# A feed-forward whose quarter products move behind six plain chunks and grow from three pairs to five

## The reference, cut to what matters

```python
def conv_gated_ffn(x, w_up, w_gate, conv_w, conv_b, w_down):
    u = x @ w_up
    g = causal_dwconv(x @ w_gate, conv_w, conv_b)
    return (jax.nn.silu(g) * u) @ w_down
...
ffn = conv_gated_ffn(x, ffn_w_up[i], ffn_w_gate[i], ffn_conv_w[i], ffn_conv_b[i], ffn_w_down[i])
ple = jax.nn.sigmoid(x @ ple_w_gate[i]) * (p[i] @ ple_w_proj[i])
x = layer_norm(DN_ALPHA * x + ffn + ple, ln_ffn_g[i], ln_ffn_b[i])
```

## Time and profile before

| what | value |
|---|---|
| median of 3 runs | 1742.17 us (1739.85 to 1743.65) |
| the profiled execution | 1736.82 us |
| its span | 1735.0 us |
| TensorE busy | 1722.2 us |
| VectorE busy | 1149.9 us |
| ScalarE busy | 898.0 us |
| DMA moved | 214.27 MB, mean 123 GB/s |

### The profile page before, as it was taken

How to read it: one execution, slowest core, us unless ns; L and a number is a source line. 1 busy time by engine, 2 the same in 40 slices (tenths; PEclk the granted TensorE clock), 3 DMA queues, 4 the chain that set the end, 5 groups by cost and what they waited for, 6 DMA issues and landing times.

```text
span 1735.0 us, 24407 instructions
## 1 busy us (share of the span) xinstructions
PE 1722.2 (99%) x9933; PEld 1430.8 (82%) x9933; DVE 1149.9 (66%) x1814; ACT 898.0 (52%) x1410; POOL 42.7 (2%) x53
## 2 busy tenths in 40 slices
PE   9999999999999999999999999999999999999999
PEld 7887999888888897777779999888898866778766
DVE  6778897644443464877697888543378866656664
ACT  7789666433332254666574665332265354534542
POOL 0000200000000000000100000000000000000000
PEclk9999999999999999999999999999999999999999
DMA  5483456755446554411124565332323221223111
GB/s 217 137 228 97 122 150 219 236 170 169 132 151 193 139 167 133 110 49 62 61 97 146 184 182 163 104 98 98 97 63 116 87 79 54 70 89 98 61 61 49
DMA packets 67247, 214.27 MB, mean 123 GB/s; under 512 B 7104, under 2 KB 7360, under 8 KB 67136
## 3 DMA queue, kind: packets, MB, share of 16 engines
q1 hardware_dynamic: 56384, 170.77, 30.2%
q0 software_dynamic: 10752, 41.95, 9.6%
HBM read 208.50 MB, written 44.04 MB: 146 GB/s over the span
## 4 chain that ended last, share of the span: by engine, by line
PE 89%; DVE 5%; ACT 4%; DMA 1%; issue 1%; SPq 0%; DVEq 0%; ACTq 0%
PE bank L620 88%; ACT tmp L1439 1%; DMA wraw<-in_wstream 1%; DVE wl L2194 1%; DVE tmp L2185 1%; ACT wh L1439 1%; ACT taps L1439 1%; PE bank L1384 0%; DVE XL L2194 0%; DVE sbl L2194 0%; DVE HL L2194 0%; ACT Y L1439 0%; ACT XH L1439 0%; DVE X L2182 0%; DVE sqr L2185 0%
## 5 line engine op out<-in xcount | busy, mean ns | idle before, releaser
L620 PE MATMUL bank<-XH,wh 128*128 128x512 f32 (+1 forms) x1424 | 526.8, 370 | 3.1 <-DVE wl L2194 1.1
L620 PE MATMUL bank<-XH,wl 128*128 128x512 f32 (+1 forms) x1424 | 517.0, 363 | 0.0
L620 PE MATMUL bank<-XL,wh 128*128 128x512 f32 (+1 forms) x1424 | 516.9, 363 | 0.0
L2194 DVE TENSOR_TENSOR wl<-wraw,wh 128x1024 fp32r<-128x1024 f32 (+1 forms) x296 | 358.1, 1219 | 232.7 <-ACT wh L1439 231.4
L1439 ACT ACTIVATE wh<-wraw 128x1024 fp32r<-128x1024 f32 (+1 forms) x296 | 309.6, 1052 | 286.6 <-PE bank L620 244.4
L620 PEld LDWEIGHTS bank<-XH,wh 128*128 128x128 f32 x1424 | 268.7, 189 | 56.1 <-issue 9.5
L620 PEld LDWEIGHTS bank<-XH,wl 128*128 128x128 f32 x1424 | 268.7, 189 | 43.0
L620 PEld LDWEIGHTS bank<-XL,wh 128*128 128x128 f32 x1424 | 269.0, 189 | 39.8 <-issue 0.7
L620 PE MATMUL bank<-HH,wh 128*128 128x256 f32 (+1 forms) x740 | 215.1, 333 | 0.0
L620 PE MATMUL bank<-HL,wh 128*128 128x256 f32 (+1 forms) x740 | 213.5, 331 | 1.4 <-DVE sqr L2185 1.4
L620 PE MATMUL bank<-HH,wl 128*128 128x512 f32 (+1 forms) x580 | 199.3, 344 | 0.0
(11 more groups left out here) (383 smaller groups left out, 2413.2 us busy)
## 6 DMA issues: line engine op xcount, KB each, us to landing
wraw<-in_wstream SPq DMA_DIRECT2D x258, 512.0 KB, 3.6
wraw<-tw SPq DMA_DIRECT2D x80, 256.0 KB, 3.1
tw<-in_w POOLq DMA_DIRECT2D x6, 2048.0 KB, 17.6
tw<-in_w POOLq DMA_DIRECT2D x6, 1536.0 KB, 11.9
tw<-in_w POOLq DMA_DIRECT2D x6, 1024.0 KB, 7.6
wraw<-in_wstream SPq DMA_DIRECT2D x22, 256.0 KB, 3.7
tw<-tw POOLq DMA_DIRECT2D x2, 2048.0 KB, 10.5
tw<-in_w POOLq DMA_DIRECT2D x6, 512.0 KB, 5.8
```

Of the source, the lines that this page charges most:

```text
L620: return pe.e.matmul(o, l, r, start=start, stop=stop, skip_group_check=True)
L2194: return dve.e.tensor_tensor(o, x, h.bitcast(F32), ALU.subtract)
```

## The change

In the first layer six plain chunks (0 to 5) come first, then five pairs (chunks 6 to 15), then six plain chunks (16 to 21). The second layer keeps seven pairs from the start. Two pairs more are done in quarter products; the stream grows from 309 units to 315, and the first layer's up and gate hold units 42 to 101, with the pairs in 54 to 88. In the first layer the two sets of three banks are exchanged: up uses 3 to 5, gate 0 to 2. The rows of `tw` are counted through both layers: 10 for the first and 14 for the second. The first layer's are summed in three parts (4, 3 and 3 rows, from `w_lo` 15, 36 and 44, step 1) in place of two (4 and 2), the second's as before in 6 and 8 rows, from `w_lo` 64 step 4 and 104 step 5 (before 60 and 100). The first pair's products wait for the products of chunks 4 and 5 in place of the sigmoids of the side gate. The places of the summed inputs stay the same.

```diff
-PAIRS = (3, 7)
-
-SUMMED = [(0, 0, 4, 15, 1), (0, 4, 6, 36, 1), (1, 0, 6, 60, 4), (1, 6, 14, 100, 5)]
-XS0 = 14
+BEFORE, PAIRS = (6, 0), (5, 7)
+UP_BANK = (3, 0)
+
+SUMMED = [(0, 4, 15, 1), (4, 7, 36, 1), (7, 10, 44, 1), (10, 16, 64, 4), (16, 24, 104, 5)]
...
+def chunk(layer, p):
+
+    return BEFORE[layer] + 2 * p
+
+
 def ffn_order(layer):
     out = []
+    for f in range(BEFORE[layer]):
+        out += [(f"up{layer}", k, f) for k in range(KD)] + [(f"gate{layer}", k, f) for k in range(KD)]
     for p in range(PAIRS[layer]):
-        f, (up, gate), (tu, tg) = 2 * p, (f"up{layer}", f"gate{layer}"), (f"tu{layer}", f"tg{layer}")
+        f, (up, gate), (tu, tg) = chunk(layer, p), (f"up{layer}", f"gate{layer}"), (f"tu{layer}", f"tg{layer}")
...
+def row(layer, p, g):
+
+    return 2 * (pairs_before(layer) + p) + g
+
+
+def summed_in(n):
+
+    return [q for q, (n0, n1, *_) in enumerate(SUMMED) if n0 <= n < n1][0]
...
-                sp.wait_ge(s.tw, 128 * (summed_in(layer, 2 * p + (mat[1] == "g")) + 1))
-                src = a["tw"][k // 4, layer, 2 * p + (mat[1] == "g")]
+                n = row(layer, p, mat[1] == "g")
+                sp.wait_ge(s.tw, 128 * (summed_in(n) + 1))
+                src = a["tw"][k // 4, n]
...
+        sets = [bank[b:b + 3] for b in (UP_BANK[layer], 3 - UP_BANK[layer])]
+        for f in range(f0):
+            bu, bg = bank[(2 + 2 * f) % 6], bank[gate_bank(f)]
+            if f < 3:
+                pe.wait_ge(s.pg_u, 8 * layer + 4 + 2 * f)
+            else:
+                pe.wait_ge(s.f_h, FT * layer + f - 2)
+            for k in range(KD):
+                block(f"up{layer}", k, f, bu[:, :], XH[:, k, :], XL[:, k, :], k == 0, k == KD - 1)
+            if f >= 3:
+                pe.wait_ge(s.f_conv, FT * layer + f - 2)
+            for k in range(KD):
+                block(f"gate{layer}", k, f, bg[:, :], XH[:, k, :], XL[:, k, :], k == 0, k == KD - 1)
...
-            b = bank[3 * g:3 * g + 3]
+            b = sets[g]
             if p:
                 pe.wait_ge(s.u_e, 4 * (pairs_before(layer) + p - 1) + 2 * g + 2)
+            elif f0:
+                pe.wait_ge(s.f_h, FT * layer + f0 - 1 + g)
             else:
                 pe.wait_ge(s.pg_u, 8 * layer + 4 + 2 * g)
...
+        for f in range(BEFORE[layer]):
+            feed_group(up, range(KD), [f])
+            feed_group(gate, range(KD), [f])
+            act.wait_ge(s.stream, w.done(gate, KD - 1, f))
+            bias(f, bank[gate_bank(f)])
+            silu(f)
+            high(f)
...
+        for f in range(BEFORE[layer]):
+            feed_group(up, range(KD), [f])
+            feed_group(gate, range(KD), [f])
+            taps(f, bank[gate_bank(f)])
+            product(f, bank[(2 + 2 * f) % 6])
+            low(f)
```

More of the change, by code:

```diff
@@ L799, in first_products @@
             mat = ("up", "gate")[g] + str(layer)
-            product(mat, 2 * p, 0, b[0][:, lo], plain(0, lo), True, False)
-            product(mat, 2 * p, 4, b[0][:, hi], plain(4, lo), False, True)
+            product(mat, chunk(layer, p), 0, b[0][:, lo], plain(0, lo), True, False)
+            product(mat, chunk(layer, p), 4, b[0][:, hi], plain(4, lo), False, True)
         def summed_products(g, p):
-            b = bank[3 * g:3 * g + 3]
+            b = sets[g]
             mat = ("tu", "tg")[g] + str(layer)
@@ L818, in last_product @@
             pe.wait_ge(s.xs_l, 4 * layer + 4)
-            product(("up", "gate")[g] + str(layer), 2 * p + 1, 4, bank[3 * g + 1][:, lo], sums_of(3), False, True)
+            product(("up", "gate")[g] + str(layer), chunk(layer, p) + 1, 4, sets[g][1][:, lo], sums_of(3), False, True)
         for p in range(PAIRS[layer]):
@@ L1534, in ffn, with sum_high @@
         HH = m.HH[layer]
+        sets = [bank[b:b + 3] for b in (UP_BANK[layer], 3 - UP_BANK[layer])]
+        def sum_high(j):
+            act.wait_ge(s.xs_f, 4 * layer + j + 1)
+            for k0, x in m.XSG[layer][j]:
+                ins = fn(x[:, :, 0:256], m.SF[layer][j][:, k0:k0 + x.shape[1], :], ACT.Copy)
+            ins.then_inc(s.xs_h, 1)
         for f0 in (0, 4):
@@ L1614, in ffn @@
         second_out(1, tg, last)
-        for f in range(2 * PAIRS[layer], FT):
+        for f in range(chunk(layer, PAIRS[layer]), FT):
             feed_group(up, range(KD), [f])
-            if f == 2 * PAIRS[layer]:
+            if f == chunk(layer, PAIRS[layer]):
                 pair_bias(last, 0)
@@ L2349, in ffn, with sum_low @@
         lo, hi, xs = slice(0, 256), slice(256, 512), m.SF[layer]
+        sets = [bank[b:b + 3] for b in (UP_BANK[layer], 3 - UP_BANK[layer])]
+        def sum_low(j):
+            dve.wait_ge(s.xs_h, 4 * layer + j + 1)
+            for k0, x in m.XSG[layer][j]:
+                ins = less(x[:, :, hi], xs[j][:, k0:k0 + x.shape[1], :], x[:, :, lo])
+            ins.then_inc(s.xs_l, 1)
         a11, a21, a12, a22 = (X[:, k0:k0 + 4, ts] for k0 in (0, 4) for ts in (lo, hi))
@@ L2391, in first_combined @@
         def first_combined(g, p):
-            b, (o, _) = bank[3 * g:3 * g + 3], (m.ub[layer][p], m.gb)[g]
+            b, (o, _) = sets[g], (m.ub[layer][p], m.gb)[g]
             dve.wait_ge(s.u_e, 4 * (pairs_before(layer) + p) + 2 * g + 1)
@@ L2397, in three_combined @@
         def three_combined(g, p):
-            b, (o, q) = bank[3 * g:3 * g + 3], (m.ub[layer][p], m.gb)[g]
+            b, (o, q) = sets[g], (m.ub[layer][p], m.gb)[g]
             dve.wait_ge(s.u_e, 4 * (pairs_before(layer) + p) + 2 * g + 2)
@@ L2406, in last_combined @@
             q = (m.ub[layer][p], m.gb)[g][1]
-            dve.wait_ge(s.stream, w.done(("up", "gate")[g] + str(layer), KD - 1, 2 * p + 1))
-            tt(q[:, lo], bank[3 * g + 1][:, lo], q[:, lo], ALU.subtract).then_inc(s.u_c, 1)
+            dve.wait_ge(s.stream, w.done(("up", "gate")[g] + str(layer), KD - 1, chunk(layer, p) + 1))
+            tt(q[:, lo], sets[g][1][:, lo], q[:, lo], ALU.subtract).then_inc(s.u_c, 1)
+        for f in range(BEFORE[layer]):
[4 more added lines that the diff above has]
+            low(f)
         for p in range(PAIRS[layer]):
-            f = 2 * p
+            f = chunk(layer, p)
             if p:
@@ L3225, in weight_sums @@
     def weight_sums(part):
-        layer, n0, n1, at, step = SUMMED[part]
-        t1, t3, t4, t2 = (a["tw"][t, layer, n0:n1].rearrange("n p c -> (n p) c") for t in range(4))
-        w11, w12, w21, w22 = (a[n][layer, n0:n1].rearrange("n p c -> (n p) c") for n in ("w11", "w12", "w21", "w22"))
+        n0, n1, at, step = SUMMED[part]
+        t1, t3, t4, t2 = (a["tw"][t, n0:n1].rearrange("n p c -> (n p) c") for t in range(4))
+        w11, w12, w21, w22 = (a[n][n0:n1].rearrange("n p c -> (n p) c") for n in ("w11", "w12", "w21", "w22"))
         done = 8 * part
@@ L3236, in gpsimd_program @@
     for i in (1, 3):
-        for part in ((0,), (1, 2, 3))[i // 2]:
+        for part in ((0,), range(1, len(SUMMED)))[i // 2]:
             weight_sums(part)
```

61 lines of the change are left out of this document (33 added, 28 removed).

## The result

The changed kernel takes 1754.46 us (median of 5 runs, 1748.82 to 1756.43), the kernel before beside it 1740.73 us; the ratio is 1.0083 (95% interval 1.0066 to 1.0100). Five further runs of the same kernel, beside more runs of the kernel before, gave 1.0102 (1.0085 to 1.0119). It is slower by 14 us, and by 20 us in those further runs, where the forecast was +3.1 us with a range that ended at 1751. The profiled execution took 1756.43 us, its span is 1754.6 us against 1735.0. The spans differ by 19.6 us and so by more than the first medians do, since the profiled execution of before (1736.82 us) was faster than all five of its runs, and this one was the slowest of its five.

The account below looks back on a forecast made before the run. TensorE was taken to bound the kernel. Saved columns -3.2, old entry gap -1.4, new entry +1.1 and additions +6.6 gave +3.1 us: 1745.3 us from a median of 1742.17, range 1738 to 1751.

Parts of the forecast that it names:

- What bounds the kernel: Whole run: TensorE, busy 1722.2 of 1735.0 us; other engines' work costs time only where TensorE starts to wait for it.
- saved columns: First layer's pairs: each saves 1.60 us against two plain chunks; five in place of three save 3.20 us.
- what the pairs add: More splits, combinations and tails on ScalarE and VectorE beside TensorE; they fit in spare time, costed at nothing.
- the banks: Exchanged banks in the first layer: products waited for are over before the pair's products start; cost nothing.
- the exit: From pair 4 to a plain chunk: the same waits as the old exit, which cost nothing.
- The entry: Start of pairs: old gap of 1.4 us goes; new one behind chunk 5 costs 1.1 us (0 to 3).
- The weight sums beside the pairs: Layer 1's sums in pairs 1 to 4: three additions at 2.2 us each, 6.6 us (4.2 to 9); copies 0.
- (c): Rival: DMA bounds pairs 1 to 4, 0.37 us a unit; +6.5 us, 1748.7 us, up to 1751; chance 0.20.
- (a): Rival: buffers cover late landings in the pairs and the new entry is free; -4.6 us, 1737.6 us; chance 0.17.
- (b): Rival: additions fall mostly on parts of a pair without a tight drain, 1 us each; 1741.7 us; chance 0.28.
- (d): Rival: the entry behind chunk 5 costs 4 us or more on top, some 1748 us; chance 0.05.
- The signs: Expected in the trace: 1 us gap in first pair, 1 to 3 us in pairs 2, 3, 4; DMA share near 0.9.

Follow-up runs that it names:

- experiment 2: Changed kernel with layer 1's weight sums moved behind the first layer's pairs and the first layer's second and third sum parts joined; 1732.30 us, ratio 0.9969.
- experiment 6: Changed kernel with ScalarE's drain of up's summed products put ahead of the weight split it stood behind; 1747.53 us, ratio 1.0054.
- experiment 5: Changed kernel with layer 1's first sum part cut in two parts of 3 rows, 768 KB an operation; 1742.17 us, ratio 1.0019.
- experiment 9: Changed kernel with 24 matmuls on unused data ahead of TensorE's wait in each of the first layer's five pairs; 1752.88 us, ratio 1.0086.

## Why the prediction was wrong

The spans moved by +19.6 us where the sum had +3.1, 16.5 more. Three terms make up 16.3 of that: the additions 13.1 in place of 6.6, the lower clock 6.2 in place of nothing, the entry 4.74 in place of 1.1.

- **What bounds the kernel; saved columns; what the pairs add; the banks; the exit.** Held. Undisturbed pairs run without a gap (experiment 2), and the sum of the terms gave -3.9 us for a span that moved by -4.5.
- **The entry.** The old gap went, as said. The new one has exactly the links predicted. Without a sum it measures 0.6 to 0.74 us (1.1 predicted, with a landing of 3.6 us where it was 3.0). With one it measures 4.74, above the upper end of 3 us, which came from a landing of 5.4 us; here it was 6.99. The step that failed is the overlap: I put the end of the last sum at about 325 us, called it a tail and charged the entry as if none stood beside it. Its last addition was issued at 320.41 us and landed at 329.3, and the transfer of 323.37 us ran beside it for all but its last microsecond. The upper end was taken from additions of 512 KB, and this one had 768.
- **The weight sums beside the pairs.** That late transfers stall TensorE at the last product of up held, and the count of three additions too. The term of the sum that was mis-sized is the one for an addition: 2.2 us (1.4 to 3) against 2.93, 5.06 and 5.10. Three things were wrong in it. The landing was taken from the end of pair 2, where TensorE was already in a plain chunk and asked for little: 9.5 us; between pairs it was up to 12.55. And lateness was reckoned for one transfer, while with three raw buffers each late one delays the issue of the next: the chain before the gap of 404.84 us holds three transfers behind one another (10.31, 7.76 and 11.69 us). And the slack behind a late split was reckoned with the drain and two combinations, 1.3 us; in pairs 2 and 3 VectorE has 2.0 us of product and taps in between, and it was that order, not the drain's, that ended last (experiment 6). Taking the middle between 1.4 and 3 weighed a 512 KB addition as heavily as the 1.5 MB one that the change puts there.
- **The clock.** Missing from the sum altogether. The trace of before shows no granted clock under 1.00 behind its longest gap, 1.39 us; in the changed kernel it is 0.50 behind each of the four gaps, for 2.9 to 3.9 us of work. The length of the gap alone does not decide: the clock fell behind 1.85 us in experiment 5 and stayed up behind 1.90 us in experiment 6 (pair 0) and behind 3.26 us in experiment 9, where added matmuls stood just ahead of it. The Trainium skill ("TensorE: Matmul & The Clock Gate", Part 1: The HAM clock gate) says that an idle array falls back to 1.2 GHz and needs sustained work to return. The changed kernel's trace agrees, with 64 matmuls in 13.9 us in place of 7.7, while 3.26 idle us in experiment 9 brought no fall. A forecast with stalls of 3 us in it should have carried such a term.
- **The rivals.** (c) named the side and the place, and gave 0.37 us a unit from the engines' total capacity, +6.5 us. That too was the wrong measure: experiment 5 moves the same bytes and loses a third as much. (a) is what the kernel does once the sums are out of the way. (b) had 1 us for an addition, and none came near it. (d), given 0.05, is part of what happened: the entry cost 4.74 us. The chance of slower, 0.40, was too low: both dated rows, the halved flow beside an addition and the spacing of 11.5 us, spoke for it, and I let the middle of a range stand against them.
- **The signs.** Most came: chunks 10.88 us apart with no gap at 263 us, a gap in pair 0 and one in each of pairs 2, 3 and 4, released by a combination into `sqr` or `third`, SyncE never waiting for `tw` there. The DMA share was 0.72, 0.98, 0.83 and 0.81 in pairs 1 to 4 where I had about 0.9. So the places were right, and the sizes were not.

## What to carry over

Before a stage with a denser stream is moved or lengthened, list the background transfers that are dated by the same counter: here a schedule in units of the stream ran twice as fast through pairs as through plain chunks. Cost a late transfer by following the ring of buffers for three turns, with the landing measured under the demand of the new place. When the last of them ends decides too: its date moves by some microseconds from one execution to the next. Follow both engines' order behind a late split, since moving one engine's work leaves the other's in the way. Long accumulating transfers belong beside work that asks for little; in halves they cost less here, though why is not shown. Other dates in the table of the sums were worth over 20 us.

## What the runs showed of the hardware

Beside an addition of 1.5 MB from HBM to HBM and the copy behind it, stream transfers of 256 KB took 7.9 us (median of 8) in place of 3.0; beside a later addition one took 12.55. Of the same 7.86 MB in sums, three additions and two copies held the 16 engines for 33.4 us, five copies for 19.9 us, and the copies left gaps of at most 1.13 us. Operations of 768 KB, each waiting for the one before to land, moved as many bytes in the same 76 us (7.84 MB), and the gaps behind pair 0 were 4.2 us in place of 13.1. TensorE's clock, once down, stayed at 0.50 for 2.9 to 3.9 us of matmuls in the changed kernel.
